# Projections moved beside the sample's mixing, and a new table for the expert slots

## What is computed

```python
h = rms_norm(x, norm_mix_g)
proj = h @ w_in                               # 1024 -> 2592 columns
y_r, new_shift, new_wkv = rwkv7_group(...)    # token shift, low-rank gates, delta-rule recurrence
y_a, new_k, new_v = swa_group(...)            # window attention, sink logit
x = x + concat([y_r, y_a]) @ w_out
x = x + peer_ffn(rms_norm(x, norm_ffn_g))     # 8 heads x 16 of 128^2 experts for every row
y = rms_norm(x, norm_final_g)
```

## Time and profile before

| | us |
|---|---|
| median of 3 runs | 4259.82 |
| the runs | 4251.76 to 4260.77 |
| profiled execution, its time | 4251.79 |
| its span, first to last instruction | 4250.0 |
| mean granted TensorE clock | 0.864 of 2.4 GHz |
| busy: TensorE, VectorE, ScalarE, GpSimd | 3255, 2906, 1418, 1435 |

### The profile page before, as it was taken

How to read it: one execution, slowest core, us unless ns; L and a number is a source line. 1 busy time by engine, 2 the same in 40 slices (tenths; PEclk the granted TensorE clock), 3 DMA queues, 4 the chain that set the end, 5 groups by cost and what they waited for, 6 DMA issues and landing times.

```text
span 4250.0 us, 44182 instructions
## 1 busy us (share of the span) xinstructions
PE 3255.1 (77%) x14236; PEld 1821.3 (43%) x14236; DVE 2905.9 (68%) x5934; ACT 1418.3 (33%) x4074; POOL 1435.1 (34%) x1158
## 2 busy tenths in 40 slices
PE   9996836887787787869786877788778868786656
PEld 5554533452545253526352544354344525452222
DVE  1003355759776977697679767876887597769765
ACT  1001102433352435233523352344244323523323
POOL 0000002424343344334333433343344243424554
PEclk9997667998889888979887989798989988898879
DMA  4102227999899899989997999799989997999998
GB/s 190 52 38 82 86 74 289 398 401 375 316 401 409 322 367 413 409 319 375 413 390 312 389 406 391 313 391 412 385 334 399 397 379 315 399 381 362 422 422 370
DMA packets 223286, 1413.08 MB, mean 332 GB/s; under 512 B 25619, under 2 KB 34323, under 8 KB 72134
## 3 DMA queue, kind: packets, MB, share of 16 engines
q0 software_dynamic: 165888, 1208.03, 70.4%
q1 hardware_dynamic: 55878, 190.35, 11.7%
q10 hardware_dynamic: 1296, 11.94, 0.7%
HBM read 1391.06 MB, written 20.41 MB: 332 GB/s over the span
## 4 chain that ended last, share of the span: by engine, by line
DVE 32%; PE 26%; DMA 14%; ACT 6%; issue 5%; POOL 1%; another core or an unknown queue 0%; DVEq 0%; SPq 0%; POOLq 0%; PEldq 0%; ACTq 0%
DVE ex_rows L1495 14%; PE mx_ps L1469 10%; DMA ex_rows<-experts,ex_expert_c 9%; PE mx_ps L1213 4%; DVE ex_x2c L1505 2%; DMA mx_fac<-w_q 2%; DMA mx_ex<-w_out 2%; DVE mx_pqb L1313 2%; DVE mx_fac L1314 2%; PE mx_ps L996 1%; DVE mx_pqb L1311 1%; PE mx_ps L1003 1%; PE mx_ps L960 1%; ACT ex_diag L1451 1%; PE mx_ps L1196 1%
## 5 line engine op out<-in xcount | busy, mean ns | idle before, releaser
L1432 POOL DMA_INDIRECT ex_rows<-experts,ex_expert_c x1152 | 1433.8, 1245 | 2781.9 <-PE mx_ps L1469 1283.6
L1469 PE MATMUL mx_ps<-ex_rows,ex_diag 128*128 128x512 f32 x3096 | 1650.8, 679 | 365.0 <-ACT ex_diag L1451 353.2
L1495 DVE CUSTOM_DVE_ANT_0 ex_rows<-ex_rows,ex_tnc 128x1024 f32<-128x1024 f32 x1152 | 1375.5, 1222 | 222.4 <-DMA ex_rows<-experts,ex_expert_c 206.5
L1469 PEld LDWEIGHTS mx_ps<-ex_rows,ex_diag 128*128 128x128 f32 x3096 | 628.2, 215 | 1227.8 <-issue 1223.3
L1441 ACT ACTIVATE ex_coef<-ex_coef 128x1 f32<-128x1 f32 x1152 | 222.9, 202 | 1549.4 <-DVE ex_coef L1495 1533.8
L1505 DVE SCALAR_TENSOR_TENSOR ex_x2c<-ex_rows,ex_coef,ex_x2c 128x1024 f32<-128x1024 f32 x378 | 485.3, 1284 | 136.5 <-ACT ex_coef L1444 129.4
L1444 ACT ACTIVATE ex_coef<-ex_coef,ex_gate_c 128x1 f32<-128x1 f32 x1152 | 283.7, 285 | 9.7
L1451 ACT ACTIVATE ex_diag<-cn_ident,ex_coef 128x128 f32<-128x128 f32 x774 | 283.3, 392 | 9.3
L260 PE MATMUL psP<-pj_w_in_sb,pj_hT 128*128 128x432 f32 x768 | 279.6, 526 | 0.0
L229 DVE TENSOR_SCALAR pj_proj_sb<-psP,pj_rstd_a 128x432 f32<-128x432 f32 x27 | 18.0, 668 | 277.7 <-PE psP L260 243.7
L260 PEld LDWEIGHTS psP<-pj_w_in_sb,pj_hT 128*128 128x128 f32 x768 | 145.4, 190 | 130.1 <-issue 130.1
(11 more groups left out here) (293 smaller groups left out, 3945.5 us busy)
## 6 DMA issues: line engine op xcount, KB each, us to landing
mx_fac<-w_q SPq DMA_DIRECT2D x54, 512.0 KB
mx_ex<-w_out SPq DMA_DIRECT2D x36, 512.0 KB
mx_ex<-w_q SPq DMA_DIRECT2D x36, 512.0 KB
ex_rows<-experts,ex_expert_c POOLq DMA_INDIRECT x1152
mx_p_cur<-w_q SPq DMA_DIRECT2D x27, 512.0 KB
mx_xs<-w_q SPq DMA_DIRECT2D x27, 512.0 KB
proj_rows<-pj_proj_sb ACTq DMA_DIRECT2D x9, 1296.0 KB, 4.7
mx_p_cur<-proj_rows SPq DMA_DIRECT2D x9, 1296.0 KB, 8.7
```

The costliest lines, as they stand in the source:

```text
L1432: pool.indirect_dma_start(rows[:, g % RING, :], None, A["experts"], bass.IndirectOffsetOnAxis(expert_c[:, s:s + 1], 0))\
L1469: last = pe.matmul(bank(6 + c), diag[:, n % DIAGS, :], up[:, r, c * 512:(c + 1) * 512], start=n == 0, stop=n == len(ON_PE) - 1)
L1495: dve.tensor_tensor_reduce(out=down[:, r, :], in0=down[:, r, :], in1=tnc[:, :], scale=1.0, scalar=0.0, op0=ALU.mult, op1=ALU.add, accum_ou ...
```

## The change

1. `project` becomes `prepare`, inside the sample's set of buffers. It transposes and scales all nine tiles (the eight prompt tiles' `hT` and `rstd` are kept in SBUF, in `W`), but multiplies and stores only the sample's tile. `w_in` is loaded by column groups; groups 2 to 5 lie in buffers that `mix` uses later, groups 0 and 1 stay.
2. The 48 other projections (six groups of eight tiles, 8 matmuls each) run in the sample's block, at the marks of a table of their own, `PROJECTION_STAGES`. All go through PSUM bank 7: a projection waits until ScalarE has copied the one before. ScalarE copies, stores the 128 x 432 piece, and loads groups 2 to 5 again when a buffer is through.
3. Bank 7 has to be free for that: the sample's outputs move to banks 3 and 6, its state updates use bank 2 alone (for each sample TensorE now waits for the sum of the one before), and the gate products wait for `y_summed`.
4. `STAGES` has other numbers, and TensorE gets a call `slots.upto(5)` between the low-rank products and its wait for the sigmoid.
5. The copies of the prompt's shift row, keys and values move to the first turn, and the sample's shifted rows are loaded without the row above them.

```diff
-def project(nc, A, C):
+def prepare(nc, A, C, W, spare, ps):
...
+            load(0)
             sp.dma_start(ident[:, :], A["ident"]).then_inc(const_loaded.sem, 16)
             sp.dma_start(gain[:, :], A["norm_mix_col"]).then_inc(const_loaded.sem, 16)
...
+            for g in range(PGROUPS):
+                for at, n, buf in parts[g]:
+                    sp.dma_start(buf, w_in[:, at:at + n, g * PG:(g + 1) * PG]).then_inc(w_in_loaded[g].sem, 16)
+                if g < 2:
+                    load(g + 1)
+            for j in range(3, TILES):
+                load(j)
...
+            transposes(0)
+            transposes(1)
+            for g in range(PGROUPS):
+                pe.wait_ge(w_in_loaded[g].sem, 16 * len(parts[g]))
+                for k in range(KC):
+                    last = pe.matmul(psP[:, g, 0:PG], hT_s[:, k, :], w_of(g, k), start=k == 0, stop=k == KC - 1)
+                last.then_inc(proj_done.sem, 1)
+                transposes(g + 2)
+            transposes(TILES - 1)
...
-STAGES = ((6, 2, 0.5), (7, 4, 0.5),
-          (16, 19, 0.4),
-          (25, 16, 0.4),
-          (28, 7, 0.2),
-          (38, 21, 0.3),
-          (42, 5, 0.7),
-          (48, 9, 0.8),
-          (59, 17, 0.0),
-          (67, 13, 0.0),
-          (71, 4, 0.3),
-          (MARKS + 1, 1, 0.5), (MARKS + 2, 0, 0.5), (MARKS + 3, 5, 0.5), (END, 5, 0.5))
+STAGES = ((7, 3, 0.3),
+          (16, 21, 0.5),
+          (25, 18, 0.4),
+          (28, 7, 0.1),
+          (38, 22, 0.3),
+          (42, 7, 0.7),
+          (48, 11, 0.8),
+          (59, 16, 0.0),
+          (67, 12, 0.0),
+          (71, 2, 0.3),
+          (END, 9, 0.3))
...
+PROJECTION_STAGES = ((1, 1), (2, 1), (6, 0), (7, 3), (16, 6), (25, 6), (28, 3), (38, 9), (48, 2), (60, 8), (MARKS, 9))
...
+            slots.upto(5)
             pe.wait_ge(sig_ready.sem, sig_ready.due(t, 1))
...
             for n in range(m["maps"]):
-                slots.upto(22 + n)
+                slots.upto(22 + min(n, 3))
...
-                    if n >= 2:
-                        pe.wait_ge(s_ready.sem, s_ready.due(t, n - 1))
-                elif n:
+                if n:
                     pe.wait_ge(s_ready.sem, s_ready.due(t, n))
...
+            if sample:
+                pe.wait_ge(y_summed.sem, y_summed.due(t, 1))
             pe.matmul(bank(2), loraT[:, P:2 * P], g2a[:, :], start=True, stop=False)
...
+            def projections_tensor(pe):
+                def products(parts):
+                    for i in parts:
+                        g, u = divmod(i, PROMPT_TILES)
+                        if g >= 2:
+                            pe.wait_ge(w_next[g % 2].sem, 16 * (g // 2))
+                        if i:
+                            pe.wait_ge(proj_copied.sem, i)
+                        for k in range(KC):
+                            last = pe.matmul(ps[:, 7, 0:PG], W["hT"][:, u, k, :], W["w"][:, g % 2, k, :],
+                                             start=k == 0, stop=k == KC - 1)
+                        last.then_inc(proj_out.sem, 1)
+                return Projections(products)
+
+            def projections_scalar(act):
+                def copies(parts):
+                    for i in parts:
+                        g, u = divmod(i, PROMPT_TILES)
+                        act.wait_ge(proj_out.sem, i + 1)
+                        if i >= 3:
+                            act.wait_ge(proj_stored[i % 3].sem, 16 * (i // 3))
+                        act.activation(pbuf[:, i % 3, :], ps[:, 7, 0:PG], ACT.Copy,
+                                       scale=W["rstd"][:, u + 1:u + 2]).then_inc(proj_copied.sem, 1)
+                        act.wait_ge(proj_copied.sem, i + 1)
+                        act.dma_start(proj[P + u * P:2 * P + u * P, g * PG:(g + 1) * PG], pbuf[:, i % 3, :])\
+                           .then_inc(proj_stored[i % 3].sem, 16)
+                        if u == PROMPT_TILES - 1 and g + 2 < PGROUPS:
+                            act.dma_start(W["w"][:, g % 2, :, :], A["w_in"].rearrange("(k p) n -> p k n", p=P)
+                                          [:, :, (g + 2) * PG:(g + 3) * PG]).then_inc(w_next[g % 2].sem, 16)
+                return Projections(copies)
...
             @block.tensor
             def _(pe):
                 pe.wait_ge(ones_ready.sem, 1)
-                mix_tensor(pe, 0, m, none)
-                route_tensor(pe, 0, none)
+                slots = projections_tensor(pe)
+                mix_tensor(pe, 0, m, slots)
+                route_tensor(pe, 0, slots)
+                slots.finish()
```

More of the change, by code:

```diff
@@ L264, in _ @@
-            transposes(0, 0, 0, True)
-            transposes(1, 1, 0)
-            pe.wait_ge(hT_ready.sem, 2)
-            pe.wait_ge(dve_evac.sem, 3)
-            pe.wait_ge(act_evac.sem, 3)
-            for k in range(KC):
-                pe.wait_ge(w_in_loaded[k].sem, 16)
-                for g in range(PGROUPS):
-                    last = pe.matmul(psP[:, g, 0:PG], hT[:, 0, k, :], w[:, k, g * PG:(g + 1) * PG],
-                                     start=k == 0, stop=k == KC - 1)
-                    if k == KC - 1:
-                        last.then_inc(proj_done.sem, 1)
@@ L384, in upto, with projection_table, __init__, finish @@
             self.experts.upto(self.mark)
+PROJECTIONS = PROMPT_TILES * PGROUPS
+PROJECTION_STAGES = ((1, 1), (2, 1), (6, 0), (7, 3), (16, 6), (25, 6), (28, 3), (38, 9), (48, 2), (60, 8), (MARKS, 9))
+def projection_table():
+    upto, first, done = [0], 1, 0
+    for last, parts in PROJECTION_STAGES:
+        upto += [round(done + parts * (m - first + 1) / (last - first + 1)) for m in range(first, last + 1)]
+        first, done = last + 1, done + parts
+    assert done == PROJECTIONS
+    return upto
+PROJECTIONS_UPTO = projection_table()
+class Projections:
+    def __init__(self, run):
+        self.run, self.done = run, 0
+    def upto(self, mark):
+        end = max(self.done, PROJECTIONS_UPTO[mark])
+        self.run(range(self.done, end))
+        self.done = end
+    def finish(self):
+        self.upto(MARKS)
 class Alone:
@@ L1043, in state_product @@
                     for o in range(2):
-                        last = pe.matmul(ps[half(o), m["st_banks"][n % 2], q * HD:(q + 1) * HD], G[half(o), n % 4, q, :],
+                        last = pe.matmul(ps[half(o), 2, q * HD:(q + 1) * HD], G[half(o), n % 4, q, :],
                                          m["S"](m["column"](n))[half(o), q, :],
@@ new lines, in mix_and_route @@
+            proj_stored = [flag(f"rows_stored{n}", 16) for n in range(3)]
+            def projections_tensor(pe):
[11 more added lines that the diff above has]
+                return Projections(products)
@@ L1371, in _ @@
             def _(act):
-                mix_scalar(act, 0, m, none)
-                route_scalar(act, 0, none)
+                slots = projections_scalar(act)
+                mix_scalar(act, 0, m, slots)
+                route_scalar(act, 0, slots)
+                slots.finish()
+                for n in range(3):
+                    act.wait_ge(proj_stored[n].sem, 16 * len(range(n, PROJECTIONS, 3)))
             @block.vector
```

218 lines of the change are left out of this document (97 added, 121 removed).

## The result

The changed kernel takes 4331.16 us (median of 4 runs, 4320.60 to 4338.64) against 4255.79 for the kernel before (4 runs beside it): a ratio of 1.0172, 95% interval 1.0154 to 1.0190. It is slower by 1.7%; the forecast was 4110 us. Its profiled execution spans 4331.0 us at a mean clock of 0.878.

The account below looks back on a forecast made before the run. No single engine was taken to bound the kernel: TensorE the first block, a three-engine chain the sample's block, VectorE, TensorE and DMA by stretches the turns. 4250.0 - 90 (front) - 53 (turns) = 4107 span; predicted 4110 us, range 4035 to 4185.

Parts of the forecast that it names:

- First block: `project`, to 338 us before: only the sample's 48 products and the transposes stay, ending at 62 us (58 to 75).
- First VectorE operation about 14 us later: Head of the sample's block: its first VectorE operation was to follow about 14 us after the block's start.
- 48 x 8 x 0.728: Sample's block: the 48 added projections cost 280 us of TensorE at full clock.
- some 0.9 us: Sample's block: a projection directly following another waits 0.9 us for the shared bank's copy, about 23 times, 21 us.
- What hides it, and the clock: Sample's block: 92 us of projections hidden in TensorE's idle times, and 30 us (0 to 46) gained from a higher clock.
- up to 10 us, nothing if they landed early: Turns, marks 29 to 49 under full DMA: four more dots, each gathered row costing 2.5 us of DMA.
- the savings: Each turn: 3 at the head, 4.9 at marks 6 to 8, 3.7 in top-k, 4.2 on TensorE; 15.8 us saved.
- The one that was to end slower: Rival 3, sample's block: projections run at 1.2 GHz, another 5.8 us each, 4390 us; chance 0.06.
- the fourth: Rival 4, turns: the table does nothing and early adds before the sigmoid cost a few us a turn, 4190 us; chance 0.05.
- rival 1: Front as computed, turns unchanged: rows moved under full DMA cost what the others give back, 4165 us; chance 0.22.
- 4107 + 1.8 + 8: Forecast span, plus the profiled execution's 1.8 us above its span and its 8 us below the median; given as 4110.
- where 90 were to be gained: Front, first and sample's blocks together: the second block was to end at 539 us instead of 629, minus 90 us.

Follow-up runs that it names:

- the trial got 28 back: Mended front with its nine score projections moved to the block's end, plus alternating PSUM banks 6 and 7 from the 21st projection: 4174.81 us, ratio 0.9817.
- the last one: Mended front, late projections, two banks and the table with four dots later, against the kernel before: 4163.88 us, ratio 0.9787; with pairs of weights added, 4180.75 us.

## Why the prediction was wrong

It was 224 us off by the profiled spans (4331.0 against 4107), 103 in the front and 121 behind it.

1. *First block, "I take 62 us (58 to 75)".* 78.6, outside the range. SyncE's order was read but x of tile 3 was not followed: it is loaded behind all of `w_in`, and TensorE, which works in written order, waits 10.3 us for it between two column groups. The trial with the loads moved ended the block at 67.0.
2. *"First VectorE operation about 14 us later".* 46.7: the step of the front that failed most. That `xs` loses one row was read in the diff and costed at nothing. 127 rows cost 30.6 us against 112 and 15.
3. *Projections, "48 x 8 x 0.728" and "some 0.9 us" for the bank.* Both right at clock 1.00: 5.8 and 0.8. Below it they were not, 308.1 us in all for 280. The bank had been taken as given at 21 us; the trial got 28 back, with nine more projections in the tail.
4. *What hides it, and the clock.* Right up to the gate products (203 us, forecast 198 to 213) and at the end (63.8, 63). Wrong in the heads' scores and attention's end: 30 to 39 us over. The forecast counted on a gain from a higher clock in the scores and on 4 us hidden. The clock did rise, from 0.50 to 0.72, and TensorE's own work got 4 us of it; but the projections ran at that clock too, 687 ns a record instead of 530, 13 us more for five. The second cause is a sentence of the forecast: what ScalarE holds back at a copy "is mostly needed by TensorE next". It was needed, and late by that very copy: exponentials whose input was there (in the head shown, for 8 us) stood behind it, and TensorE waited 10.9 us for five of them (0.4 before). The Trainium skill's rule on PSUM queues ("TensorE: Matmul & The Clock Gate", "A second HAM failure mode: psum-queue depth-cycling") spoke of this kind of loss, but not of this place: in the tail, where the one bank is waited for 16 times, the clock was 1.00, and the low clock was in the scores, where it had been low before.
5. *The turns, "up to 10 us, nothing if they landed early" for four dots in the stretch with full DMA.* This is the step that turned the sign: a price of at most 10 us a turn, where 18 was measured. The mechanism behind the price was wrong, not only its size: rows were costed as bytes of DMA, and bytes are the same. What changed is who gets them. Dots that come earlier free places in the ring of rows earlier, so the gathers always have work while the weights stream, and take their share from it: +18 us in marks 43 to 48 of the turn shown, and 122 us more of waits for the router's weights over the eight turns. Of the savings, the TensorE-bound stretch and top-k were right (4.1 and 3.6 for 4.2 and 3.7). The first 60 us gave 1.8 for 7.9, and the mixed stretch grew by 3.4 for 1.2. The earlier trace rows had been read as VectorE's head; with VectorE's work gone as forecast, TensorE's adds were in the chain, 9.9 us for the four that had been counted at 8 and set against 4.4 us of the saving.
6. *The rivals.* The one that was to end slower, projections at 1.2 GHz, is out as a whole: 1.00 in the long stretches of them. A part of it came true in the scores. The early adds of the fourth cost nothing with the old table; with the new one they are in the chain. The first came nearest, with rows moved under a full DMA that cost what the others give back, but put that at nothing gained and not at a loss. None of the four had the weights' stream in it, though the earlier trace rows showed a share of 1.00 over 134 us.
7. *The last sums.* 4107 + 1.8 + 8 is 4117 and not 4110, and rival 1's sum is 4170 and not 4165. Neither matters beside 224.

The table is the larger part (+62 us), the front the smaller (+14, where 90 were to be gained). With three causes taken away (127 rows, x behind `w_in`, projections among the heads) the front gives 50 us. The second bank brings it to 78; that this is near the 90 is luck, since the 90 were forecast with one bank.

What stays open: what the early adds cost with the new table by themselves, why four dots later leave the router's part at 53 us and not at 44, and how pairs cost 16 us in the kernel before and 17 in the last one.

## What to carry to other kernels

Where DMA is full, a share of 1.00 says nothing about who gets it: list the streams, their row sizes and which of them the path waits for, before work that feeds the other one is moved next to it. Look at the row count of every transfer that a diff touches. Fill gaps of TensorE with long work only where no short chain across engines runs beside it, and look at what stands behind the copy of its result on the engine that copies; elsewhere put it in a row, with two banks. When work is taken from the engine that bounds a stretch, ask which engine's order bounds it then.

## What the runs showed of the hardware

- Two queues with work were served one packet for one: 2,494 and 2,418 packets in 65 us, 279 and 135 GB/s with 8 KB and 4 KB rows; 308 and 308 in 10 us with most of the weights in 8 KB rows.
- While a load of 127 rows (905 KB) was under way, the core's DMA moved 21 to 30 GB/s for 29 us; with 112 and 15 rows the whole stretch ran at 259 GB/s.
- One core's DMA held 415 GB/s over these 65 us, with reads from two queues. The Trainium skill ("DMA: Bandwidth & Descriptors", "Specifications") gives some 358 GB/s as the limit of HBM for a core; this trace goes above it, as the earlier trace rows did.
